# Cross attention on split tiles: single-pass products, and two query tiles between the units

## The reference

```python
def memory_cross_attention(xn, memn, wq, wkv, wo):
    b, s, _ = xn.shape
    q = (xn @ wq).reshape(b, s, X_HEADS, X_HEAD_DIM)
    k, v = jnp.split(memn @ wkv, 2, axis=-1)
    ...
    sc = jnp.einsum('bshd,bmhd->bhsm', q, k).astype(jnp.float32) * (X_HEAD_DIM ** -0.5)
    p = jax.nn.softmax(sc, axis=-1).astype(v.dtype)
    o = jnp.einsum('bhsm,bmhd->bshd', p, v).reshape(b, s, D_MODEL)
    return o @ wo
```

## Time and profile before

| | us |
|---|---|
| median of 3 runs | 1619.0 (1618.93 to 1619.3) |
| profiled execution | 1618.77 |
| its span | 1617.0 |
| PE busy | 1580.7 (98%) |
| DVE busy | 841.6 (52%) |
| ACT busy | 583.0 (36%) |
| POOL busy | 547.3 (34%) |

### The profile page before, as it was taken

One profiled execution on the slowest core, in us unless ns is written; L12 is line 12 of the kernel. 1 busy time (PEld: TensorE's weight loads), 2 busy tenths in 40 slices (PEclk: granted clock), 3 DMA queues, 4 the chain that ended last, 5 costly groups with the idle time before them and its releaser, 6 DMA issues.

```text
span 1617.0 us, 19949 instructions
## 1 busy us (share of the span) xinstructions
PE 1580.7 (98%) x7386; PEld 1197.5 (74%) x7386; DVE 841.6 (52%) x1419; ACT 583.0 (36%) x955; POOL 547.3 (34%) x239
## 2 busy tenths in 40 slices
PE   7999999999999999999999999999999999999997
PEld 6888779887888888887876768888877885444543
DVE  6447586135744466245777786344243654433434
ACT  4227455243322234415532342343243333112213
POOL 4441227622444435840432124455424410000000
PEclk9999999999999999999999999999999989999998
DMA  5331224522333333630322113344313449999991
GB/s 190 103 92 40 78 92 143 154 68 84 92 92 104 92 91 109 185 102 24 99 72 68 37 52 95 103 122 128 103 52 92 149 185 372 419 423 422 421 418 72
DMA packets 52786, 235.93 MB, mean 146 GB/s; under 512 B 6240, under 2 KB 7136, under 8 KB 48096
## 3 DMA queue, kind: packets, MB, share of 16 engines
q1 hardware_dynamic: 48960, 222.60, 40.0%
q0 software_dynamic: 2016, 7.34, 1.1%
q10 hardware_dynamic: 1728, 4.87, 0.9%
HBM read 230.59 MB, written 4.19 MB: 145 GB/s over the span
## 4 chain that ended last, share of the span: by engine, by line
PE 92%; DVE 5%; issue 1%; ACT 1%; DMA 0%; SPq 0%; DVEq 0%; ACTq 0%
PE G L1821 72%; PE O L1821 7%; PE S L1821 6%; PE TR L1821 5%; PE TR L1932 2%; PE G L2391 1%; DVE sq L1084 1%; DVE U L1055 1%; DVE sumsq L1019 0%; DVE U L1798 0%; DVE arena L1442 0%; DMA w_ring<-in_stream_dram 0%; ACT cm_hi L595 0%; DVE sumsq L1728 0%; DVE RB L1390 0%
## 5 line engine op out<-in xcount | busy, mean ns | idle before, releaser
L544 POOL TENSOR_TENSOR lo_ring<-w_ring,hi_ring 128x1024 fp32r<-128x1024 f32 x219 | 533.6, 2438 | 770.9 <-ACT hi_ring L579 770.8
L579 ACT ACTIVATE hi_ring<-w_ring 128x1024 fp32r<-128x1024 f32 x219 | 231.4, 1058 | 564.2 <-PE G L1821 560.7
L1821 PE MATMUL G<-xa_hi,hi_ring 128*128 128x512 f32 x928 | 375.6, 405 | 9.6 <-DVE xa_lo L1146 9.0
L1821 PE MATMUL G<-xa_hi,lo_ring 128*128 128x512 f32 x928 | 362.6, 391 | 0.0
L1821 PE MATMUL G<-xa_lo,hi_ring 128*128 128x512 f32 x928 | 362.3, 390 | 0.0
L1821 PEld LDWEIGHTS G<-xa_hi,hi_ring 128*128 128x128 f32 x928 | 175.1, 189 | 48.0 <-issue 11.9
L1821 PEld LDWEIGHTS G<-xa_lo,hi_ring 128*128 128x128 f32 x928 | 175.2, 189 | 37.7 <-issue 2.4
L1821 PEld LDWEIGHTS G<-xa_hi,lo_ring 128*128 128x128 f32 x928 | 174.8, 188 | 37.2
L1821 PE MATMUL G<-yb_hi,hi_ring 128*128 128x512 f32 x388 | 153.1, 395 | 0.0
L1821 PE MATMUL G<-yb_hi,lo_ring 128*128 128x512 f32 x388 | 151.1, 389 | 0.0
L1821 PE MATMUL G<-yb_lo,hi_ring 128*128 128x512 f32 x388 | 151.0, 389 | 0.0
(11 more groups left out here) (351 smaller groups left out, 2494.4 us busy)
## 6 DMA issues: line engine op xcount, KB each, us to landing
w_ring<-in_stream_dram SPq DMA_DIRECT2D x219, 512.0 KB, 3.5
arena<-in_w_gu_dram SPq DMA_DIRECT2D x16, 2048.0 KB, 12.3
ex_rings<-in_w_dn_dram SPq DMA_DIRECT2D x40, 512.0 KB, 16.1
ex_low<-in_w_gu_dram SPq DMA_DIRECT2D x8, 2048.0 KB, 18.7
ex_rings<-in_w_gu_dram SPq DMA_DIRECT2D x8, 2048.0 KB, 16.3
arena<-in_w_dn_dram SPq DMA_DIRECT2D x16, 512.0 KB, 14.6
sq<-in_w_dn_dram SPq DMA_DIRECT2D x8, 512.0 KB, 18.6
X<-in_x_in_dram SPq DMA_DIRECT2D x8, 256.0 KB, 5.4
```

The costliest lines, as they stand in the source:

```text
L544: nc.gpsimd.tensor_tensor(lo_ring[:, s, :], w_ring[:, s, :], hi_ring[:, s, :], ALU.subtract).then_inc(low, 1)
L579: nc.scalar.activation(hi_ring[:, m % RING, :], w_ring[:, m % RING, :], ACT.Copy).then_inc(high, 1)
L1821: return nc.tensor.matmul(*args, **kw)
```

## The change

Queries, keys, values and transposed probabilities are kept as pairs of float32r tiles, and each full product becomes three single-pass ones: high x high, high x low, low x high. Per unit of scores 12 products in place of 4, per tile of values 6 in place of 2.

- Keys: DVE writes the float32 tile into `U` (`xk_f`), ACT copies it to `xk_hi` (`key_high`), DVE subtracts in place (`key_low`).
- Values: ACT copies from PSUM with the scale (`values_high`), DVE subtracts from PSUM (`xv_lo`).
- Queries: DVE writes `q_f`, which lies in the memory of `yb_lo`; ACT copies to `yb_hi` (`query_high`), DVE subtracts in place (`query_low`). On ACT, the copy of query j stands behind `unit_done` of query j+1 (for 5 and 7: behind its own).
- Probabilities: ACT copies `TR` to `xPT` (float32r), and DVE subtracts it from `TR` (`prob_low`). The next transposes into `TR`, and the values, now wait for that subtraction.
- Order on PE: six query tiles; scores 0 to 3; transposes 0 to 3, each with half a query tile behind it (6, 6, 7, 7); values 0; scores 4, 5, 6; transposes 4; scores 7; values 1, transposes 5, values 2, transposes 6, values 3, transposes 7; values 4 to 7.

The views, and PE, from the diff:

```diff
-        xk, xv = A(0, KT, MEM), A(2048, 2, D)
-        xP, xPT = A(4096, 2, T), [A(5120, 4, T), A(7168, 4, T)]
+        xP, xPT = A(4096, 2, T), [arena_r[:, n:n + 4 * T].rearrange("p (a b) -> p a b", a=4) for n in (5120, 7168)]
+        xk_hi = arena_r[:, 0:2048].rearrange("p (a b) -> p a b", a=KT)
+        xv_hi = arena_r[:, 2048:4096].rearrange("p (a b) -> p a b", a=MT)
+        xk_f = U[:, 0:4, :].rearrange("p a (b c) -> p (a b) c", c=MEM)
+        xk_lo = U_r[:, 0:4, :].rearrange("p a (b c) -> p (a b) c", c=MEM)
+        xv_lo = U_r[:, 4:8, :].rearrange("p (m a) c -> p m (a c)", m=MT)
+        xPT_lo = [cm_lo[:, 0:4 * T].rearrange("p (a b) -> p a b", a=4), xa_lo[:, 4:8, :]]
...
-                for j in range(KT):
+                for j in range(6):
                     tile(f"q{i}", j, xa_hi, xa_lo)
...
-                            ins = mm(score(base + u, h * MEM, (h + 1) * MEM), U[:, j, t * P:(t + 1) * P],
-                                     xk[:, j, :], start=d == 0, stop=d == 1)
+                            if t == 0:
+                                pe.wait_ge(xq_low, i * KT + j + 1)
+                            rows = slice(t * P, (t + 1) * P)
+                            for n, (q, k) in enumerate(((yb_hi, xk_hi), (yb_hi, xk_lo), (yb_lo, xk_hi))):
+                                ins = mm(score(base + u, h * MEM, (h + 1) * MEM), q[:, j, rows], k[:, j, :],
+                                         start=d == 0 and n == 0, stop=d == 1 and n == 2)
...
-                        ins = mm(x_o(j), xv[:, m, j * P:(j + 1) * P], xPT[hp][:, 2 * h + m, :],
-                                 start=m == 0, stop=m == MT - 1)
+                        for n, (v, p) in enumerate(((xv_hi, xPT), (xv_hi, xPT_lo), (xv_lo, xPT))):
+                            ins = mm(x_o(j), v[:, m, cols], p[hp][:, 2 * h + m, :], start=m == 0 and n == 0,
+                                     stop=m == MT - 1 and n == 2)
                     ins.then_inc(o_full, 1)
+
+                def probs_t(u):
+                    if u:
+                        pe.wait_ge(xpt_low, i * 8 + u)
+                    transposed(base + u, xP, 4)
...
-                for u in range(8):
-                    transposed(base + u, xP, 4)
-                    if u + 4 < 8:
-                        scores(u + 4)
-                    if u >= 4:
-                        values(u - 4)
+                for u in range(4):
+                    probs_t(u)
+                    half = range(u % 2 * (KT // 2), (u % 2 + 1) * (KT // 2))
+                    piece(f"q{i}", 6 + u // 2, xa_hi, xa_lo, half)
+                values(0)
+                for u in range(4, 7):
+                    scores(u)
+                probs_t(4)
+                scores(7)
+                for u in range(5, 8):
+                    values(u - 4)
+                    probs_t(u)
                 for j in range(4, KT):
                     values(j)
```

ACT around the queries, and DVE from the first unit on:

```diff
+                for j in range(6):
+                    unit_done(f"q{i}", j)
+                    if j:
+                        query_high(j - 1)
+                query_high(5)
...
+                for u in range(4):
+                    copy_of(u)
+                    if u == 0:
+                        one(3)
+                    if u == 1:
+                        unit_done(f"q{i}", 6)
+                    if u == 2:
+                        query_high(6)
+                unit_done(f"q{i}", 7)
+                query_high(7)
...
+                def query_low(j):
+                    dve.wait_ge(xq_high, i * KT + j + 1)
+                    nc.vector.tensor_tensor(yb_lo[:, j, :], q_f[:, j, :], yb_hi[:, j, :],
+                                            ALU.subtract).then_inc(xq_low, 1)
...
+                for j in range(6):
+                    query(j)
+                    if j:
+                        query_low(j - 1)
+                query_low(5)
...
+                def prob_low(u):
+                    hp, t = divmod(u, TT)
+                    part = slice(t * P, (t + 1) * P)
+                    dve.wait_ge(pt_ready, base + u + 1)
+                    nc.vector.tensor_tensor(xPT_lo[hp][:, :, part], TR[:, :].rearrange("p (a b) -> p a b", b=P),
+                                            xPT[hp][:, :, part], ALU.subtract).then_inc(xpt_low, 1)
...
+                normalise(base, 2, MEM, xP)
+                top(3)
+                for u in range(4):
+                    if u < 3:
+                        normalise(base + u + 1, 2, MEM, xP)
+                    prob_low(u)
+                    if u == 1:
+                        query(6)
+                    if u == 2:
+                        query_low(6)
+                query(7)
+                query_low(7)
+                for u in range(4, 7):
+                    top(u)
+                normalise(base + 4, 2, MEM, xP)
+                for u in range(4, 8):
+                    prob_low(u)
+                    if u == 4:
+                        top(7)
+                    if u < 7:
+                        normalise(base + u + 1, 2, MEM, xP)
+                    if u > 4:
                         low_of(x_o(u - 5), yb_hi[:, u - 5, :], yb_lo[:, u - 5, :], o_free)
```

More of the change, by code:

```diff
@@ L125, in build @@
         cm_lo = sb("cm_lo", [P, 5 * T], F32R)
+        with ExitStack() as rounded:
+            U_r = rounded.enter_context(nc.sbuf_tensor("U_r", [P, KT, T], F32R))
+            arena_r = rounded.enter_context(nc.sbuf_tensor("arena_r", [P, 11264], F32R))
         U = sb("U", [P, KT, T])
@@ L158, in build @@
         lo_ring = early("lo_ring", [P, RING, D], F32R)
+        with ExitStack() as unrounded:
+            q_f = unrounded.enter_context(nc.sbuf_tensor("q_f", [P, KT, T], F32))
         yb_lo = early("yb_lo", [P, KT, T], F32R)
@@ L216, in build @@
         o_free = sem("o_free")
+        xk_high, xk_low = sem("cross_keys_high"), sem("cross_keys_low")
+        xv_high = sem("cross_values_high")
+        xq_high, xq_low = sem("cross_queries_high"), sem("cross_queries_low")
+        xpt_low = sem("cross_prob_t_low")
         dve_order = sem("dve_order")
@@ L730, in cross, with key_high, values_high, query_high @@
             def cross(i, norm):
[L731 to L735, removed]
+                def key_high(j):
+                    act.wait_ge(evac, ACC0[f"k{i}"] + j + 1)
+                    nc.scalar.activation(xk_hi[:, j, :], xk_f[:, j, :], ACT.Copy).then_inc(xk_high, 1)
+                def values_high(c):
+                    for m in range(MT):
+                        a = ACC0[f"v{i}" + "ab"[c]] + m
+                        act.wait_ge(full, a + 1)
+                        nc.scalar.activation(xv_hi[:, m, c * T:(c + 1) * T], G[:, a % BANKS, :], ACT.Copy,
+                                             scale=rcm[:, m:m + 1]).then_inc(xv_high, 1)
+                def query_high(j):
+                    act.wait_ge(evac, ACC0[f"q{i}"] + j + 1)
+                    nc.scalar.activation(yb_hi[:, j, :], q_f[:, j, :], ACT.Copy).then_inc(xq_high, 1)
+                for j in range(KT):
+                    unit_done(f"k{i}", j)
+                    if j == 2:
+                        wide_root(norm)
+                    if j:
+                        key_high(j - 1)
+                for c in range(2):
+                    for j in range(4):
+                        unit_done(f"v{i}" + "ab"[c], j)
+                        if c == 0 and j == 0:
+                            key_high(KT - 1)
+                    values_high(c)
+                for j in range(6):
[3 more added lines that the diff above has]
+                query_high(5)
                 base = SU[f"x{i}"]
@@ L2070, in scores @@
                     hp, t = divmod(u, TT)
-                    if u in (0, 2, 3, 4):
-                        pe.wait_ge(evac, ACC0[f"q{i}"] + {0: 4, 2: 5, 3: 6, 4: 8}[u])
+                    if u == 0:
+                        pe.wait_ge(xk_low, (i + 1) * KT)
                     scores_free(base + u)
+                    if u in (2, 3):
+                        pe.wait_ge(evac, ACC0[f"q{i}"] + u + 3)
                     for h in range(2):
```

44 lines of the change are left out of this document (28 added, 16 removed).

## The result

The changed kernel takes 1632.7 us (median of 6 runs, 1629.4 to 1634.6) against 1619.0 (median of 6 runs, 1618.5 to 1620.6). The ratio is 1.0083, with a 95% interval of 1.0073 to 1.0093. The forecast was 1628.4, with a range of 1621 to 1634: sign and range hold, and the size is 4.3 us short of the 13.7 that the change costs.

A forecast was written before the change was run, and what follows sets the result against it. TensorE (PE), busy 98% of the span, was taken to bound the kernel. New waits of 10.3 us, less 0.2 of before and 5.3 of work, gave +4.7 per cross attention, +9.4 for both: 1619.0 to 1628.4, range 1621 to 1634.

The forecast's parts named there:

- What decides: DVE against GpSimd: Query subtractions behind query tiles: GpSimd holds DVE's subtraction of two SBUF tiles, 2.90 us for what takes 0.7 alone.
- step 4: Transposes of unit 4, right behind scores 6: PE waits 1.9 us while DVE takes maximum 6 before normalising 4.
- steps 1 and 3: PE waits for DVE's low query parts: 2.4 us ahead of transposes 0, 2.0 us inside the scores of unit 4.
- step 5: Units 5 to 7: DVE chains make PE wait 0.5, twice 0.95, then 1.6 us ahead of values 4.
- The terms that the prediction put at nothing: New key and value work on DVE and ACT, and the second attention's rotation angles delaying ACT's first query copy: no cost.
- fourth rival: PE's clock falls to half in steps 4 and 5: up to +4 us per attention, 1629 to 1636; chance 6%.
- the 5.3: PE work saved per cross attention in us, with the transposes at 0.44 each; 5.1 without.
- third rival: Normalising 3 falls under GpSimd, transposes of unit 3 come 1.7 us late: +3.4 for both attentions, 1632; chance 10%.
- Step 2: Transposes of units 0 to 3 with halves of query tiles: 3.16 us of PE per unit, DVE fits, no wait.
- Fewer PE steps: Scores 1.44 us a unit for 1.72, values 1.36 a tile for 1.72: 5.1 us less PE work per attention.
- first rival: Softmax stays covered by PE, all waits vanish and only the work saving is left: 1608.5 us; chance 7%.

The follow-up runs named there:

- normalising first: Against the changed kernel: in each attention's second half DVE normalises unit u+1 ahead of the low part of unit u's probabilities (u = 4, 5, 6); 1628.8 us, ratio 1.0058.
- the split alone: Split products with the PE order of the kernel before, DVE normalising ahead of the low part throughout; 1626.6 us, ratio 1.0046 against the kernel before.
- the copies first: Against the changed kernel: ACT copies queries 5, 6 and 7 to their high parts ahead of rounding the next ring unit; 1626.1 us, ratio 1.0043.
- the roundings away: Against the kernel with query copies ahead of rounding: ACT's rounding of three ring units (behind query tiles 5, 6, 7) moved later; 1621.7 us, ratio 1.0022.
- all orders anew: Against the changed kernel: split and moved query tiles kept, PE, DVE and ACT orders in each cross attention rewritten; 1612.5 us, ratio 0.9963 against the kernel before.
- the order alone: The kernel before, full-precision products, given the changed kernel's order on PE, ACT and DVE without copies and subtractions; 1625.1 us, ratio 1.0041.

## Why the prediction was right, and where it fell short

**The mechanism.** "What decides: DVE against GpSimd" and the chains of step 4 and 5 are shown. The runs took the hold away (steps 1 and 3), turned it onto another instruction (the first maximum's scaling), shortened the chain (step 5) and kept it with nothing split (step 4). Each moved by what the steps say, to a few tenths of a microsecond. The terms that the prediction put at nothing were nothing: between 40.20 us and the first scores, with the stages of keys and values in it, PE lost 0.08 us against before; and in the second attention ACT's first query copy waited 6.04 us for DVE's angles, and PE for nothing.

Three things in it don't hold as written. The row at 256.54 that it calls a subtraction is a running sum (`sumsq<-sumsq,sq`); it reads two SBUF tiles too, and the query subtraction was held in the same way (2.48 us for 0.69, ending 0.55 us behind GpSimd). For the fourth rival it has PE "nearly idle" at the lowered clock, but its row for 1326 to 1328 has PE busy for 1.68 of 2.00 us. And its sum comes to 4.8 us per attention with the 5.3, not 4.7.

**The number.** 1632.7 lies in the range, but above the 1625 to 1631 that the forecast itself was given. It sits at the third rival's 1632, and that is chance: the rival didn't happen. What lifted the time was mostly two terms that the sum doesn't have, a fall of the clock and the start, told below.

**The terms.** In the second attention, where no row shows a lowered clock, start by start against the forecast: scores 0 to transposes 0 8.12 for 8.15; units 0 to 3 12.88 for 12.64; values 0 to transposes 4 9.60 for 9.58; to transposes 5, 6 and 7 3.82, 2.81, 2.81 for 3.75, 2.75, 2.75; to values 4 2.04 for 2.02; from there to `o1` 5.58 for 5.44. In sum 47.66 for 47.0. The term that was too small is the pace behind transposes, for the most part; the largest miss is in units 0 to 3: 3.2 a unit, not 3.16. After each four transposes the first two products start 0.31 apart and some of the others 0.23, not 0.227. Twice 0.65 is 1.3 of the missing 4.3 us.

**Step 2 and the third rival.** Normalising 3 got in before GpSimd: its two scalings began at 352.12 and some 0.3 later, GpSimd at 352.52. The margin of 0.1 us that I had given it held in both attentions, and the rival didn't happen.

**The fourth rival, in part.** "If it fell to half for steps 4 and 5" put the fall in the thin end of the attention. The clock did fall, in another place: behind the 2.21 us wait of step 1, in the first attention only. Stretches of 2 us (length, busy PE, PEld, DVE, ACT, POOL, granted clock, DMA share, GB/s):

```profile
341.00:343.00 2.00, 0.00 (x0) 0.00 (x0) 1.90 (x7) 2.00 (x10) 0.00 (x0) 1.00 0.33 133
343.00:345.00 2.00, 1.85 (x7) 1.66 (x8) 1.62 (x7) 1.37 (x6) 0.00 (x0) 0.51 0.00 0
345.00:347.00 2.00, 2.00 (x7) 1.60 (x6) 1.31 (x4) 0.81 (x4) 0.00 (x0) 0.64 0.00 0
347.00:349.00 2.00, 2.00 (x12) 1.69 (x11) 0.00 (x0) 0.43 (x1) 0.00 (x0) 1.00 0.00 0
...
732.00:734.00 2.00, 0.91 (x6) 0.88 (x7) 1.86 (x9) 1.83 (x9) 0.00 (x0) 1.00 0.00 0
734.00:736.00 2.00, 2.00 (x10) 1.61 (x10) 1.84 (x6) 1.29 (x5) 0.00 (x0) 1.00 0.00 0
```

From 343 to 347 PE is busy and stands at the lower of its two levels, 1.2 GHz, for some 3.4 us (worked out from the 0.51 and 0.64). Transposes 1 come 4.79 us after transposes 0 in place of 3.26: 1.5 us. The second attention waits the same 2.21 us and shows 1.00. I had weighed only low activity in a stretch, and not what may follow a wait.

**The start.** 1.65 us come before the first scores, and nearly all of them ahead of anything that the change touches: 1.57 are there when PE is at 40.20 (38.63 before). Most of the cause shows in DVE's scaling of the first norm, one row of the changed kernel and one of the kernel before:

```profile
27.37 3.17 DVE L1083 TENSOR_SCALAR sq<-ident,rc 128x128 f32<-128x128 f32 x4
```

```profile
27.01 0.87 DVE L1028 TENSOR_SCALAR sq<-ident,rc 128x128 f32<-128x128 f32 x4
```

In the changed kernel this scaling was held by GpSimd, whose operation began at 28.08. PE waited 1.0 us for it. Ahead of the scaling PE was 0.37 us late (26.62 for 26.25), behind it 1.6 (31.16 for 29.57). All these kernels have equal code there. In the four others whose scaling was held (3.4 us) PE loses 1.4 to 1.5 us across it, and in the two whose scaling took 0.88 it loses nothing; the first start their scores 0.7 to 1.2 us late, the second 0.3 and 0.6. So the hold costs 1.2 us of the 1.65. What decides whether GpSimd meets the scaling, by the build or by the execution, and where the smaller part comes from, stays open: each kernel has one profile.

**The swap behind the attentions.** Before, the clock also fell between 850 and 856, behind a wait of PE of 1.89 us that ended at 849.80, and not at the same place after:

```profile
850.00:852.00 2.00, 2.00 (x8) 1.59 (x8) 1.97 (x4) 0.00 (x0) 1.52 (x1) 0.76 0.37 150
852.00:854.00 2.00, 2.00 (x7) 1.51 (x6) 0.36 (x1) 0.00 (x0) 0.00 (x0) 0.50 0.70 195
```

That gives 1.6 us back, and a longer stretch at the low level around 1340 takes 1.4 again. Neither was in the forecast, and they cancel. That they cancel is luck.

**The sum.** 9.4 forecast + 1.3 pace + 1.5 clock + 1.65 start = 13.85 against 13.8. This is the one profiled execution, laid out after the fact; other executions of the kernel took 1629.4 to 1634.6. The term "Fewer PE steps" was right: three tiles of values, from 380.11 to 384.19, take 1.36 us each. The first rival (softmax covered, 1608.5) was no illusion as a bound: with other orders the same products reach 1612.5.

## What to carry to other kernels

Before work is taken off the engine that bounds, lay the chain of the engine that becomes next end to end, start to start, through every queue that it passes: here 10.6 us of PE work went, some 20 of waiting came, and order alone gave 17 of them back (47.66 to 39.05, twice). An instruction moved out of a hold's way may hand the hold to its successor (0.17 us became 2.09), so move the engine that holds as well: the copies early gave 2.8 us in an attention, and rounding three ring units later, which nobody waits for (from the one attention to the other it stays 340.78 us), a further 1.2. A loop through a single buffer (transposes, copy, subtraction: 2.0 us) sets the pace; put the work that it doesn't need, normalising, outside of it, and keep one filler for its last turn.

## What the runs showed of the hardware

- After a wait of 2.21 us ahead of transposes 0, PE's clock fell for some 3.4 us in four of six attentions (the changed kernel's first, both with normalising first, the first with the split alone) and not in the other two, at a cost of 1.0 to 1.6 us. After waits of 1.46 or 0.27 in the same place it never fell, in four. It also fell near the end of the attention, around the wait ahead of values 4: once with the copies first (first attention) and once with the roundings away (second). The place of the fall between 850 and 856 before says the same: all eight profiles have its wait of 1.9 us, and the clock fell behind it in four (before, copies first, normalising first, split alone). Equal waits stand in both attentions of a kernel too, so a wait alone doesn't decide it, and what does was not tested. It may be behind the spread between runs of one kernel (1629.4 to 1634.6; 1620.5 to 1626.5).

```profile
372.00:374.00 2.00, 1.01 (x3) 0.87 (x4) 1.76 (x3) 0.70 (x2) 0.00 (x0) 0.84 0.00 0
374.00:376.00 2.00, 2.00 (x6) 1.51 (x6) 0.13 (x1) 0.34 (x1) 0.00 (x0) 0.50 0.00 0
376.00:378.00 2.00, 2.00 (x9) 1.59 (x8) 0.69 (x1) 0.62 (x2) 0.00 (x0) 0.81 0.00 0
```

  These are the stretches with the copies first: PE half busy, then at half clock. The kernel with all orders anew and the one with the order alone show no fall in either attention.
- A DVE instruction on 128 x 2 numbers is held by GpSimd to the end of its operation (2.09 us for 0.17), and a subtraction of two SBUF tiles of 128 x 512 some 0.5 us beyond it (2.48 us for 0.69), while a reduction from PSUM begun beside such an operation isn't (0.69).
